# Two latent query tiles share one product with the values in the attention of a two-layer hybrid backbone

## The reference, cut to what matters

```
def _block_attention(q, k, v, scale):
    ...
        s = jnp.einsum('bqhd,bkhd->bhqk', qblk, k).astype(jnp.float32) * scale
        p = jax.nn.softmax(s, axis=-1).astype(v.dtype)
        return jnp.einsum('bhqk,bkhd->bqhd', p, v)
```

## Time and profile before

| | us |
|---|---|
| median of 3 runs | 1039.73 |
| the runs | 1037.18 to 1041.11 |
| span of the profiled execution, first to last instruction | 1037.1 |
| TensorE busy in it | 949.1 |
| VectorE busy | 348.7 |
| ScalarE busy | 251.1 |
| DMA of weights and rows, 313.66 MB | mean 302 GB/s |
| attention, layer 0 | 143.3 to 218.0 |
| attention, layer 1 | 647.6 to 722.2 |

### The profile page before, as it was taken

One profiled execution on the slowest core, in us unless ns is written; L12 is line 12 of the kernel. 1 busy time (PEld: TensorE's weight loads), 2 busy tenths in 40 slices (PEclk: granted clock), 3 DMA queues, 4 the chain that ended last, 5 costly groups with the idle time before them and its releaser, 6 DMA issues.

```text
span 1037.1 us, 13937 instructions
## 1 busy us (share of the span) xinstructions
PE 949.1 (92%) x5397; PEld 468.3 (45%) x5397; DVE 348.7 (34%) x886; ACT 251.1 (24%) x600; POOL 132.0 (13%) x152
## 2 busy tenths in 40 slices
PE   4999989999999999888779998999999999988895
PEld 3445545655433433333344554566554333433342
DVE  2240176531752221111151004755148212221227
ACT  2120145421511111111151103554141211110124
POOL 4121000001111111110033100000121111111101
PEclk8999999999999999999889999999999999999999
DMA  9951366676999999999993026651959999999994
GB/s 345 394 224 62 142 249 239 244 298 270 367 378 382 401 394 393 399 414 415 391 351 118 21 81 249 262 210 63 423 223 337 372 392 392 396 415 411 416 400 165
DMA packets 58569, 313.66 MB, mean 302 GB/s; under 512 B 6826, under 2 KB 9094, under 8 KB 27520
## 3 DMA queue, kind: packets, MB, share of 16 engines
q1 hardware_dynamic: 50208, 288.54, 71.2%
q0 software_dynamic: 7424, 21.01, 5.9%
q10 hardware_dynamic: 864, 3.15, 0.7%
HBM read 300.01 MB, written 17.26 MB: 306 GB/s over the span
## 4 chain that ended last, share of the span: by engine, by line
PE 66%; DMA 22%; DVE 4%; issue 3%; ACT 2%; SPq 1%; POOL 1%; ACTq 0%; POOLq 0%; DVEq 0%
DMA arena<-in_w_up 15%; PE psum L1098 12%; PE psum L1506 8%; PE psum L1376 8%; PE psum L1164 7%; PE psum L1348 4%; PE psum L1339 4%; PE psum L1011 3%; PE psum L1446 3%; DMA arena<-in_w_ada 3%; PE psum L1476 2%; PE psum L1458 2%; PE psum L1110 2%; DMA arena<-token_rows,row_i 2%; PE psum L1401 1%
## 5 line engine op out<-in xcount | busy, mean ns | idle before, releaser
L1098 PE MATMUL psum<-arena 128*64 128x512 f32 x480 | 218.2, 603 | 22.9 <-DMA arena<-in_w_up 22.7
L1101 PE MATMUL psum<-arena 128*64 128x512 f32 x480 | 218.6, 604 | 0.0
L1098 PEld LDWEIGHTS psum<-arena 128*64 128x64 f32 x480 | 64.5, 139 | 165.3 <-issue 163.0
L1164 PE MATMUL psum<-arena 128*64 128x512 f32 x480 | 112.7, 608 | 2.9 <-ACT arena L1677 0.9
L2119 DVE SCALAR_TENSOR_TENSOR arena<-arena,psum 64x512 f32<-64x512 f32 (+2 forms) x32 | 22.9, 714 | 253.9 <-ACT arena L1671 253.9
L1506 PE MATMUL psum<-arena 128*128 128x384 f32 x256 | 84.0, 488 | 0.6 <-PE psum L1506 0.6
L1376 PE MATMUL psum<-arena 128*128 128x384 f32 x256 | 83.4, 487 | 0.6 <-PE psum L1376 0.6
L1671 ACT ACTIVATE arena<-psum 64x512 f32<-64x512 f32 (+2 forms) x32 | 19.7, 617 | 259.7 <-PE psum L1101 238.6
L1101 PEld LDWEIGHTS psum<-arena 128*64 128x64 f32 x480 | 64.5, 139 | 0.0
L1376 PEld LDWEIGHTS psum<-arena 128*128 128x128 f32 x256 | 48.3, 190 | 34.7 <-issue 1.8
L1506 PEld LDWEIGHTS psum<-arena 128*128 128x128 f32 x256 | 48.2, 190 | 34.5 <-issue 2.1
(11 more groups left out here) (317 smaller groups left out, 1195.8 us busy)
## 6 DMA issues: line engine op xcount, KB each, us to landing
arena<-in_w_gate SPq DMA_DIRECT2D x64, 1024.0 KB, 27.3
arena<-in_w_up SPq DMA_DIRECT2D x64, 1024.0 KB, 27.9
arena<-in_w_down SPq DMA_DIRECT2D x64, 1024.0 KB, 29.0
arena<-in_w_ada SPq DMA_DIRECT2D x24, 2048.0 KB, 7.9
arena<-in_w_in SPq DMA_DIRECT2D x6, 2048.0 KB, 18.2
arena<-in_w_out SPq DMA_DIRECT2D x4, 2048.0 KB, 7.9
arena<-expert_rows SPq DMA_DIRECT2D x12, 512.0 KB, 10.9
arena<-in_w_in SPq DMA_DIRECT2D x2, 1664.0 KB, 13.2
```

Of the source, the lines that this page charges most:

```text
L1098: ins = nc.tensor.matmul(bank[b][0:MAIN, :], hg[:, k, 0:MAIN], row(wg[half], k), start=(k == 0), stop=(k == KD - 1))
L1101: ins = nc.tensor.matmul(bank[b][MAIN:P, :], hg[:, k, 0:MAIN], row(wu[half], k), start=(k == 0), stop=(k == KD - 1))
L1164: ins = nc.tensor.matmul(bank[6][MAIN * j:MAIN * j + MAIN, :], hidT[:, c, 0:MAIN], down_row(w[half], c)[:, 512 * j:512 * j + 512], start=( ...
```

## The change

The two latent tiles of a pair are multiplied by the values together. `values(w)` now runs only for t = 0 and for t = 2; the latter takes both latent tiles, whose turned probabilities lie in the two buffers of `probT0` and `probT`, as one streamed operand of 2 x 128 columns, and writes columns 256 to 511 of bank 6. The context tile's turned probabilities get a place of their own (`turned_place`), in half of `probT` that was unused. `outputs` follows: one operation on 128 x 256 for both latent tiles. A pair so has two shares instead of three units, 16 a layer, and the counts on `o_ready` and `o_ps` go by shares. The rounds with u mod 3 = 2 have no `values` and no `outputs`. Copies of round u now wait for the share of unit u - 3. GpSimd no longer raises `o_ready` at the start.

```diff
+SHARES = 16
...
-                sp.wait_ge(o_ready, UNITS * (l + 1) + 1)
+                sp.wait_ge(o_ready, SHARES * (l + 1))
...
-            pool.sem_inc(o_ready, 1)
...
-                pool.wait_ge(o_ready, UNITS * l + 1)
+                if l:
+                    pool.wait_ge(o_ready, SHARES * l)
...
+        def turned_place(u):
+
+            t = u % 3
+            if t == 0:
+                return probT[:, 0, 0, 0:2 * P], probT[:, 0, 0, 2 * P:3 * P]
+            return probT0[:, t - 1, :], probT[:, t - 1, 1, :]
+
+        def share_done(eng, l, w):
+
+            eng.wait_ge(o_ready, SHARES * l + 2 * (w // 3) + (1 if w % 3 == 0 else 2))
...
-                            ins = nc.tensor.matmul(bank[6][HD * i:HD * i + HD, 0:P], v, (probT[:, w % 2, 1, P * c:P * c + P] if i else probT0[:, w % 2, P * c:P * c + P]),
-                                                   start=(c == 0), stop=(c == n // P - 1))
+                            if t == 0:
+                                out, turned_rows = bank[6][HD * i:HD * i + HD, 0:P], turned_place(w)[i][:, 0:P]
+                            else:
+                                out = bank[6][HD * i:HD * i + HD, LAT:2 * LAT].rearrange("p (t n) -> p t n", t=2)
+                                turned_rows = (probT[:, :, 1, P * c:P * c + P] if i else probT0[:, :, P * c:P * c + P])
+                            ins = nc.tensor.matmul(out, v, turned_rows, start=(c == 0), stop=(c == n // P - 1))
...
-                    if u >= 1:
-                        if u >= 2:
-                            pe.wait_ge(o_ready, UNITS * l + u)
-                        if u == 11 or u == 23:
-                            ada_fold(l, 1 + u // 12)
+                    if u == 11 or u == 23:
+                        ada_fold(l, 1 + u // 12)
+                    if u >= 1 and u % 3 != 2:
+                        if u >= 3:
+                            share_done(pe, l, u - 3 if u % 3 == 0 else u - 2)
                         values(u - 1)
...
-                                pe.wait_ge(o_ready, UNITS * l + 3 * k + 4)
+                                pe.wait_ge(o_ready, SHARES * l + 2 * k + 2)
...
-                    if u >= 2:
-                        act.wait_ge(o_ready, UNITS * l + u)
-                    nc.scalar.activation(probT0[:, u % 2, 0:n + P], bank[4][:, 0:n + P], ACT.Copy).then_inc(probT_act, 1)
+                    if u >= 3:
+                        share_done(act, l, u - 3)
+                    nc.scalar.activation(turned_place(u)[0][:, 0:n + P], bank[4][:, 0:n + P], ACT.Copy).then_inc(probT_act, 1)
...
-                    v.tensor_tensor(o, bank[6][:, 0:P], probT0[:, w % 2, n:n + P], ALU.mult).then_inc(o_ready, 1)
+                    spread = turned_place(w)[0][:, n:n + P].unsqueeze(1) if t == 0 else probT0[:, :, n:n + P]
+                    at = 0 if t == 0 else LAT
+                    v.tensor_tensor(o, bank[6][:, at:at + P * m].rearrange("p (t n) -> p t n", t=m), spread, ALU.mult).then_inc(o_ready, 1)
...
-                    if u >= 2:
-                        dve.wait_ge(o_ps, UNITS * l + u - 1)
-                    v.tensor_copy(probT[:, u % 2, 1, 0:n], bank[5][:, 0:n]).then_inc(probT_dve, 1)
-                    if u >= 1:
+                    if u >= 3:
+                        share_done(dve, l, u - 3)
+                    v.tensor_copy(turned_place(u)[1][:, 0:n], bank[5][:, 0:n]).then_inc(probT_dve, 1)
+                    if u >= 1 and u % 3 != 2:
                         outputs(u - 1)
```

More of the change, by code:

```diff
@@ L2320, in outputs @@
                     kind, pair, t, n = unit(w)
-                    dve.wait_ge(o_ps, UNITS * l + w + 1)
-                    o = hT[:, 4 * kind + pair, P * t:P * t + P]
+                    dve.wait_ge(o_ps, SHARES * l + 2 * (w // 3) + (1 if t == 0 else 2))
+                    m = 1 if t == 0 else 2
+                    o = hT[:, 4 * kind + pair, 0:P] if t == 0 else hT[:, 4 * kind + pair, P:TOK]
                     if kind == 0:
-                        o = bass.AP(o.tensor, o.offset + P - 1, [list(o.ap[0]), [-1, P]])
-                    v.tensor_tensor(o, bank[6][:, 0:P], probT0[:, w % 2, n:n + P], ALU.mult).then_inc(o_ready, 1)
+                        o = bass.AP(o.tensor, o.offset + P - 1, [list(o.ap[0]), [P, m], [-1, P]])
+                    else:
+                        o = o.rearrange("p (t n) -> p t n", t=m)
+                    spread = turned_place(w)[0][:, n:n + P].unsqueeze(1) if t == 0 else probT0[:, :, n:n + P]
+                    at = 0 if t == 0 else LAT
+                    v.tensor_tensor(o, bank[6][:, at:at + P * m].rearrange("p (t n) -> p t n", t=m), spread, ALU.mult).then_inc(o_ready, 1)
                 maxes(0)
@@ L2341, in _ @@
                 dve.wait_ge(fold_ps, ADA_ROUNDS * (l + 1))
-                dve.wait_ge(o_ready, UNITS * (l + 1) + 1)
+                dve.wait_ge(o_ready, SHARES * (l + 1))
                 modulation(l, 2, 6)
```

## The result

The changed kernel takes 1032.44 us (median of 4 runs, 1029.18 to 1034.13) where the kernel before took 1039.56 (4 runs), a ratio of 0.9926 with a 95% interval of 0.9906 to 0.9946. In a later series on one chip it took 1031.96 against 1040.34, ratio 0.9919 [0.9903, 0.9936]. The forecast was 1032.6 us, with a chance of 0.68 for a gain of more than 0.5%.

The account below looks back on a forecast made before the run. Attention was taken as bound by TensorE's work plus 3.2 us of gaps a layer. Gains of 0.81 + 1.30 + 0.39 + 0.54 + 0.50 = 3.54 a layer, 7.1 in all, took 1039.73 to 1032.6 us; range 1029.8 to 1038.3.

Parts of the forecast that it names:

- blocks-only case: Rival in attention: removed waits come back elsewhere, only saved TensorE blocks pay; gain 2.9 us, time 1036.8, chance 0.14.
- The wide block: Attention's `values` on 256 columns: 1.44 us to the next block, against 1.62 for two narrow ones.
- First to third triple: Start of a layer's attention: first gains 0.81 us, second and third 0.65 each as the wait for VectorE's copy goes.
- Fourth triple: Where kind 1 begins in attention: 0.18 us from merging plus a removed wait of 0.21, gain 0.39.
- The end: Eighth triple and end of a layer's attention: delayed transposes fall into the next wait, last narrow block goes; gain 0.50 us.
- Later stages: After attention: first expert weight transfer is issued behind the last block and moves with it, so the gain is kept.
- fifth to seventh: Kind-1 triples of a layer's attention: no wait to remove, merging gives 0.18 us each, 0.54 together.
- slower case: Rival in attention: two heads' wide products no longer run side by side; time 1053.2 us, chance 0.04.
- cheap block: Rival in attention: a wide block costs no more than a narrow one; 10.1 us more gain, 1022.5, chance 0.05.
- absorbed case: Rival in the experts: the weight stream sets its own start, so nothing arrives; time 1039.7 us, chance 0.08.

Follow-up runs that it names:

- the first experiment: The changed kernel with both latent tiles multiplied by 128-column products, six pairs in one block, instead of 256-column ones; 1032.09 us, ratio 0.9937 to the kernel before.

## Why the prediction was right

**The mechanism.** Fewer blocks, and a longer block where TensorE had waited: both halves are in the trace, 3.2 us of TensorE's busy time and 3.1 of idle time. (The forecast split its sum into 2.9 and 4.2. It took the waits from start to start, 0.47 where the page of the profile counts 0.38, so the two splits are not the same measure.) The blocks-only case would have left kind-0 triples at 8.72 − 0.18 = 8.54 us; they are 8.12, without a wait. The run with two narrow blocks isolates the second half: it has the old number of products and of blocks (only VectorE's scaling is merged, which the run with two scalings shows to be worth nothing there), and its second and third triple are still 0.43 shorter than before.

**The wide block.** 1.44 forecast, 1.45 measured, and 1.46 with narrow products. The reasoning held to the hundredth: array time scales with columns, one fixed part is saved. The attribution of the fixed part to the block was loose; the two-block run shows that it depends on the neighbours, 0.31 between scores and transposes. In the change it made no difference, since the block that went stood between transposes and the modulation piece, where taking it out is worth 0.16 (kind-1 triples of 9.31 and 9.15).

**First to third triple.** 0.81 as forecast, then 0.60 for 0.65. The sum had the small scores at 0.40 and the transposes unchanged; they are 0.42 and 0.92 instead of 0.88.

**Fourth triple.** 0.49 for 0.39. I took the length of kind 1's small scores from the chain, 0.64; the timeline gives 0.55 (190.04 to 190.59 in the first experiment, and the same in the kernel before), so the old wait was 0.30 and not 0.21. Durations in the chain are cut at different points than starts in the timeline, and a wait must be taken from one of the two throughout.

**The end.** This is the step of the prediction that failed: 0.18 for 0.50. That the delay of the transposes falls into the next wait, with 0.07 left of it, was argued for ScalarE's copy alone. The chain that became late was VectorE's: scaling, reciprocals and spreading end 0.88 us after the transposes' start, and these can do without the result for 0.6. The prediction had checked this very chain in kind 0, found 0.15 us to spare, and not redone it where the scores between block and transposes are missing. The reciprocals-first run gives 0.27 of the missing 0.32 back.

**Later stages.** No stage took the gain back, as the place of the first expert issue had suggested. That the medians differ by 7.1 us, exactly the forecast, owes something to luck. The traces account for 6.35 us in the attentions, 0.7 less than the sum, and the errors of the terms partly cancel: a layer lost 0.32 at the end, 0.10 in the second and third triple and 0.04 in the fifth to seventh, and gained 0.10 in the fourth. Another 0.3 to 0.4 lie outside the span and were in no term. Two other comparisons, of the same pair and of the kernel with narrow products in one block, gave 8.4 and 7.0.

**The rivals.** The slower case (two heads no longer side by side) and the cheap block are both excluded by 1.45 us. The absorbed case is excluded by the medians, and no stretch between or behind the attentions grew beyond its scatter.

**Two slips that changed nothing.** The 44 us that the prediction gives as VectorE's share beside TensorE is, in the earlier trace rows, the busy time of TensorE's weight loads; no term uses it. And its own bounds, 1031.7 − 1.5, make 1030.2 as the lower end of the range, not 1029.8; the measured median lies above both.

## What to carry to other kernels

Before merging operations, ask which part of the gain needs the merge: here one block of twelve narrow products did nearly as well as one of six wide ones, and about half of the gain came from the block standing in front of a wait. When a chain's margin has been computed in the steady state, compute it again for the first and the last round, where the work that covers it is missing. A filler moved into a gap can bare another gap; here that ate the gain, and in two of four layers TensorE's clock fell besides. Splitting it kept the clock up and won 0.31 us a layer by the traces.

## What the runs showed of the hardware that was not expected

- A block of 0.64 us of products, put between scores and transposes of kind 1, costs 0.95 us. The 0.31 beside the products falls on the places where the array's used shape changes, 0.05 to 0.16 us each; that the shape is the cause is not shown.
- In the two kernels with the whole piece moved TensorE waits three times, 0.85, 0.70 and 0.60 us, ahead of the piece. In two of their four layers the granted clock then fell to 0.53 or 0.57 while the piece ran, and 1.86 us of work took 3.2 to 3.4; in the other two it stayed at 1.00. With the piece split, so that one half covers the 0.70, it stayed at 1.00 in both layers. The Trainium skill, page "TensorE: Matmul & The Clock Gate", section "What's actually happening", describes two levels of 1.2 and 2.4 GHz between which recent activity decides; the windows agree with a fall to the lower one.
- For float32 products of 64 stationary columns, two side by side, 128 and 256 streamed columns run at the same pace a column (1.46 and 1.45 us for a block).
